# Experts' first and third matrices laid out by four consecutive rows to a partition, in a two-layer hybrid kernel with grouped experts

## The reference, cut to what matters

```python
def _moe(h, router_w, router_b, w1, w3, w2):
    ...
    for e in range(N_EXPERTS):
        hid = jax.nn.silu(t @ w1[e]) * (t @ w3[e])
        y = y + gates[:, e:e + 1] * (hid @ w2[e])
    ...
# before it, per layer:  h = _rmsnorm(x) * (1 + scale) + shift
# w1[e], w3[e]: 1024 x 256     w2[e]: 256 x 1024
```

## Time and profile before

| | us |
|---|---|
| median of three runs | 1369.6 |
| profiled execution, its own time | 1365.57 |
| span of its profile | 1363.9 |
| PE busy in the span | 1225.5 (90%) |
| DVE / ACT / GpSimd busy | 841.9 / 477.0 / 322.9 |
| bytes moved by DMA | 234.77 MB in 125291 packets |
| of the packets, under 2 KB / under 8 KB | 77168 / 125200 |

### The profile page before, as it was taken

The page is one execution under the profiler, slowest core; times in us unless marked ns, Lnnn a source line. Parts: engine busy times, 40 slices in busy tenths (PEclk is TensorE's granted clock), DMA queues, the critical chain, the costliest instruction groups (busy, mean ns, idle before and its releaser), DMA issues.

```text
span 1363.9 us, 24844 instructions
## 1 busy us (share of the span) xinstructions
PE 1225.5 (90%) x9304; PEld 825.2 (61%) x9304; DVE 841.9 (62%) x1644; ACT 477.0 (35%) x974; POOL 322.9 (24%) x384
## 2 busy tenths in 40 slices
PE   2989999999799998699999699999999997899980
PEld 2478867847455453584854478888887555455540
DVE  5577575483566664869335677777774325576664
ACT  4000126203366551201038544444443102556541
POOL 1000009100233333100002433443443000333323
PEclk9899899899899999799999899999999998899995
DMA  9677666482999986311110000000001634599945
GB/s 365 217 247 284 213 233 219 134 304 101 319 378 324 378 287 203 125 62 62 62 62 0 31 3 3 21 3 2 3 2 64 233 106 154 200 383 378 380 132 206
DMA packets 125291, 234.77 MB, mean 172 GB/s; under 512 B 9376, under 2 KB 77168, under 8 KB 125200
## 3 DMA queue, kind: packets, MB, share of 16 engines
q1 hardware_dynamic: 114464, 200.42, 42.3%
q0 software_dynamic: 10560, 33.04, 6.8%
q10 hardware_dynamic: 176, 0.05, 0.0%
HBM read 210.42 MB, written 23.07 MB: 171 GB/s over the span
## 4 chain that ended last, share of the span: by engine, by line
PE 67%; DVE 13%; SPq 9%; DMA 5%; issue 4%; ACT 2%; POOL 1%; DVEq 0%; POOLq 0%; ACTq 0%
PE PS L2191 14%; PE PS L2157 8%; SPq L735 8%; PE PS L2336 7%; PE PS L2112 5%; PE PS L2354 3%; PE PS L2535 2%; PE PS L2085 2%; PE PS L2517 2%; PE PS L2423 2%; PE PS L2486 2%; DMA arena<-in_ada_w 2%; DVE arena L1390 2%; DVE arena L1762 2%; PE PS L2261 1%
## 5 line engine op out<-in xcount | busy, mean ns | idle before, releaser
L2336 PE MATMUL PS<-WR,arena 128*64 128x256 f32 x1536 | 180.0, 388 | 5.9 <-ACT arena L1188 4.5
L2336 PEld LDWEIGHTS PS<-WR,arena 128*64 128x64 f32 x1536 | 109.3, 139 | 61.2 <-ACT arena L1188 7.2
L2191 PE MATMUL PS<-WR,arena 128*128 128x256 f32 x480 | 111.4, 393 | 4.3 <-DVE arena L1837 4.2
L2157 PE MATMUL PS<-WR,arena 128*128 128x512 f32 x256 | 113.6, 600 | 0.0
L1390 DVE SCALAR_TENSOR_TENSOR arena<-arena,cact 128x1024 f32<-128x1024 f32 x77 | 99.4, 1291 | 12.1 <-DMA arena<-in_ada_w 6.0
L2191 PEld LDWEIGHTS PS<-WR,arena 128*128 128x128 f32 x480 | 94.0, 197 | 20.2 <-DVE arena L1837 3.4
L1640 DVE COPY WR<-arena 128x2560 f32 x48 | 71.9, 1498 | 38.5 <-issue 26.0
L2354 PE MATMUL PS<-W,arena 128*64 128x512 f32 x384 | 92.9, 604 | 0.9 <-DVE arena L1666 0.9
L923 POOL DMA_DIRECT2D expert_rows<-arena x92 | 49.7, 540 | 157.6 <-DVE arena L1674 150.8
L1172 ACT COPY WR<-arena 128x1536 f32 x48 | 71.0, 1480 | 44.8 <-issue 26.5
L2112 PE MATMUL PS<-arena,WR 128*128 128x512 f32 x192 | 85.5, 601 | 1.1 <-DVE arena L1477 1.1
(11 more groups left out here) (382 smaller groups left out, 2231.0 us busy)
## 6 DMA issues: line engine op xcount, KB each, us to landing
arena<-in_moe_w SPq DMA_DIRECT2D x96, 1024.0 KB, 13.1
arena<-in_ada_w SPq DMA_DIRECT2D x82, 512.0 KB, 4.7
WR<-in_rwkv_w_rkv SPq DMA_DIRECT2D x6, 2048.0 KB, 8.0
expert_rows<-arena POOLq DMA_DIRECT2D x92, 128.0 KB, 5.5
WR<-in_mix_w_in SPq DMA_DIRECT2D x5, 2048.0 KB, 10.5
WR<-in_mix_w_out SPq DMA_DIRECT2D x2, 2048.0 KB, 7.9
expert_rows<-arena SPq DMA_DIRECT2D x1, 4096.0 KB, 14.7
xn_rows<-WR SPq DMA_DIRECT2D x2, 2048.0 KB, 7.2
```

The costliest lines, as they stand in the source:

```text
L2157: last = mm(out, HT[:, c, b * P:(b + 1) * P], WR[:, (first_tile + half) % 2, c, :], start=(c == 0), stop=(c == KC - 1))
L2191: last = mm(out[:, n * 256:n * 256 + 256], left, right, start=(c == 0), stop=(c == 3))
L2336: last = mm(PS[rows2[h], 2 + n, 0:2 * P].rearrange("p (m f) -> p m f", m=2), XgT[:, n, c, :], w[:, :, c, cols(h)], start=(c == 0), stop=(c ...
```

## The change

The loads of w1 and w3 give a partition two runs of four consecutive rows (4 KB each), one run from each half of the 1024 features. Chunk number 4h + c then holds the features 512h + 4p + c in place of 512h + 128c + p. `turn` picks each fourth column of the gathered rows to match. Since scale and shift are now needed in the same order, SP rewrites sixteen columns of `MOD` for each layer (`reorder`): one transfer to DRAM, number by number, a wait for its landing, and one transfer back, into a part of `vecA`. ACT and DVE wait for that once in each layer. w2 and all else stay as they are.

```diff
+        mod_dram = nc.dram_tensor("mod_rows", (2 * D,), F32, kind="Internal").ap()
+        MODP = [vecA[:, 24 * (2 * layer + 1):24 * (2 * layer + 1) + 2 * KC] for layer in range(2)]
...
+            def reorder(layer):
+                sp.wait_ge(sem("mod_ready"), 2 * layer + 3)
+                sp.wait_ge(sem("sgu_in"), 32 + 32 * layer)
+                with nc.allow_non_contiguous_dma(reason="one number of each partition"):
+                    sp.dma_start(mod_dram.rearrange("(j p) -> p j", p=P), MOD[:, 2 * layer + 1, 0:2 * KC]
+                                 ).then_inc(sem("sgu_in"), 16)
+                sp.wait_ge(sem("sgu_in"), 48 + 32 * layer)
+                sp.dma_start(MODP[layer].rearrange("p (m h c) -> p m h c", m=2, h=2),
+                             mod_dram.rearrange("(m h p c) -> p m h c", m=2, h=2, c=4)).then_inc(sem("sgu_in"), 16)
...
             sp.wait_ge(*free("s4", 4))
+            reorder(0)
             sp.dma_start(y_dram[NEXP * ROWS:MAX_ITEMS * ROWS, :].rearrange("(k p) f -> p k f", p=P),
...
-                    for k, name in enumerate(("moe_w1", "moe_w3", "moe_w2")):
-                        sp.dma_start(slot[:, k * 2048:(k + 1) * 2048].rearrange("p (c f) -> p c f", c=2 if k == 2 else KC),
-                                     io[name][layer, e].rearrange("(c p) f -> p c f", p=P)
+                    for k, name in enumerate(("moe_w1", "moe_w3")):
+                        sp.dma_start(slot[:, k * 2048:(k + 1) * 2048].rearrange("p (h f) -> p h f", h=2),
+                                     io[name][layer, e].rearrange("(h p c) f -> p h (c f)", h=2, p=P)
                                      ).then_inc(sem(f"ring_in{e % SLOTS}"), 16)
+                    sp.dma_start(slot[:, UP:EXPW].rearrange("p (c f) -> p c f", c=2),
+                                 io["moe_w2"][layer, e].rearrange("(c p) f -> p c f", p=P)
+                                 ).then_inc(sem(f"ring_in{e % SLOTS}"), 16)
...
             moe(0)
+            reorder(1)
             sp.dma_start(W1L, io["rwkv_w1"][0].rearrange("(c p) f -> p c f", p=P)).then_inc(sem("lora_in"), 16)
...
+                act.wait_ge(sem("sgu_in"), 64 + 32 * layer)
                 act.wait_ge(sem("items"), layer + 1)
...
-                                                    bias=MOD[:, L, c:c + 1], scale=MOD[:, L, 8 + c:9 + c])
+                                                    bias=MODP[layer][:, c:c + 1], scale=MODP[layer][:, 8 + c:9 + c])
...
+                v.wait_ge(sem("sgu_in"), 64 + 32 * layer)
                 stage_up(0, expert(0))
...
-                        last = nc.tensor.transpose(PS[:, n + c // 2 * 4, cols(c % 2)], Xg[:, n, cols(c)], ident[:, :])
+                        last = nc.tensor.transpose(PS[:, n + c // 2 * 4, cols(c % 2)],
+                                                   Xg[:, n, :].rearrange("p (q c) -> p c q", c=4)[:, c, :], ident[:, :])
```

More of the change, by code:

```diff
@@ L1653, in turned @@
                         at = (c % 4 - 2) * P + c // 4 * ROWS
-                        last = ts(XgT[:, n, c, :], PS[:, 4 + n, at:at + ROWS], MOD[:, L, 8 + c:9 + c],
-                                  MOD[:, L, c:c + 1], ALU.mult, ALU.add)
+                        last = ts(XgT[:, n, c, :], PS[:, 4 + n, at:at + ROWS], MODP[layer][:, 8 + c:9 + c],
+                                  MODP[layer][:, c:c + 1], ALU.mult, ALU.add)
                     last.then_inc(M("xgv_hid"), 1)
```

## The result

The changed kernel takes 1374.44 us (median of 6 runs, 1370.65 to 1375.51), the kernel before 1368.74 beside it (6 runs, 1367.0 to 1371.43). The ratio is 1.0042, with a 95% interval of 1.0029 to 1.0055: longer by 0.42%, 5.7 us, where I had forecast 5.9 us less. The time lies inside the range (1359.5 to 1378.0), but on the side that I gave 0.18.

What follows compares the result with a forecast made beforehand. PE and DMA were both near their limit in the expert stages, with 6.7 us due to late weights. Terms -6.4 + 0 + 0.5 = -5.9 us took 1369.6 to 1363.7 us (-0.43%), range 1359.5 to 1378.

Steps and rivals of the forecast that it cites:

- The loads, -6.4 us: Expert stages: longer runs for w1 and w3 land weights sooner; -3.0 - 1.7 - 1.7 = -6.4 us.
- Both waits: PE waits for late weights, 3.30 us in layer 0 and 1.72 in layer 1; booked as -3.0 and -1.7 us.
- the slower item: Layer 0 item behind the late expert, 1.69 us over the pace at a lower PE clock; booked as gone.
- Rival B: Expert loops: slower item stays or experts behind the late one come late; 1366.4 us, within 0.3%; chance 0.20.
- "Cost 0" for the second `reorder`: Behind layer 0's experts: SP waits for the landing but reaches `tile(7)` in time; 0 us.
- "+0.5" for its small pieces: Gathers after layer 0: small pieces take up to 4 us, later small matrices return 1.4; +0.5 us booked.
- Rival C: Second `reorder`: 4-byte pieces take 20 us to land and delay gathers; +4 us, 1367.2 us, within 0.3%; chance 0.07.
- The return of 1.4 us: Gathers after layer 0: small matrices now come later, which can give back 1.4 us.
- "I take 0" for the turns: PE's transposes: stepped weight loads hide behind the 110 ns spacing; 0 us, upper bound +19.6 us.
- Rival A: PE's turns: stepped load is slow, transposes over 110 ns apart; 1383.3 us at 212 ns; chance 0.18.
- Rival D: Expert loops: longer runs delay an item's gathers past 10.2 us; 1381.7 us at 11 us; chance 0.05.
- The first `reorder`, 0: Ahead of the store at 223.32 us: 3 to 15 us of SP delay, some 20 us of cover; 0 us.

Runs made afterwards that it cites:

- the fourth kernel: The changed kernel with the second `reorder` moved some 250 us later, behind the loads at about 772 us: 1365.96 us, ratio 0.9986 to the kernel before.

## Why the prediction was wrong

**The loads, -6.4 us: right.** Both waits went, the slower item with them, and alone the loads gave 5.9 us. The waits themselves aren't fixed numbers: in the profiles of four kernels with the old loads (both `reorder`s alone, small reads, spread writes, small matrices moved) the late expert of layer 0 is 3.8 to 4.3 us late and none is late in layer 1, so 5.4 to 5.9 us with the slower item would be the term there in place of 6.7. Rival B (less is returned) isn't borne out by the changed kernel or by the loads alone; a trace of it shows in three later kernels, where one `up` of layer 0 waits 0.2 to 0.95 us for weights. The rule that I quoted from the Trainium skill, "DMA: Bandwidth & Descriptors", section "Why small descriptors are slow" (7% between the two lengths of run in place of 14%) would have made the sum 1.5 us smaller; the measurement of the loads alone lies between the two sums, 6.4 and 4.9 us, and its interval (3.8 to 7.9 us) excludes neither.

**"Cost 0" for the second `reorder`, and "+0.5" for its small pieces: the step that failed most.** The landing time lay within its bounds of 3 to 15 us (10.4; measured 13.7), and the way of the damage was named, small pieces beside the gathers. Its size was not: bounds of -1.4 to +4 us against 7.3 measured alone and 9.3 in the profile. I priced pieces by number, from reads of 64 bytes, and capped the delay by how much longer they would be under way. But the row of the router matrix is a read from DRAM, and this is a write to it. 2048 reads of 4 bytes held up no gather, and 128 writes of 64 bytes had landed before the gather that counts; 2048 writes of 4 bytes side by side took every gather beside them to 16.5 to 18.0 us, from 5.1 to 8.2. The gathers landed 6 to 7 us after these writes did, as if they had waited for them, and not later by the difference of two landings. Rival C had this mechanism, with its sign "a last lower gather over 9 us" (17.3), but priced it at 4 us, and so stood on the wrong side of zero. The return of 1.4 us for small matrices that come later is real, as the kernel with these alone moved shows (2.2 us off the gather), but what holds the gathers up is stronger.

**"I take 0" for the turns: the second step that failed.** The row that I leaned on, matmuls 106 ns apart behind plain weight loads of 192 ns, was taken to say that any load of about that length hides behind a spacing of 106 to 110. I had also called the contiguous load twice as fast as the plain one, while the row reads 142 against 192 ns, a third apart. The stepped load measured 209 ns, and the turn grew by 0.09 us. Four loads grew by 4 x 67 = 268 ns, and a third of that, 0.09 us, came through to PE; how the rest is hidden no row shows. The bounds (0 to 0.102 us a transpose) held the truth, 0.023 us a transpose, near their lower end. This is Rival A, with its sign (a turn over 0.6 us), at a fifth of the price that I gave it. The slowing is less than a factor of two, as that rival's "against" had it; that it would then hide was the error. The sentence from the Trainium skill, "Advanced Engine Details and Errata", section "SBUF Cachelines", which I quoted under Rival A, names a penalty for such a step, and the trace agrees, 209 ns against 142.

**Gathers in the loop (Rival D): refuted.** No item waits in either loop.

**The first `reorder`, 0: right,** by the cover of the modulation loads. The added waits of ACT and DVE show no cost: the fourth kernel has both in, and its -0.14% is what loads and turns leave.

So the two prices together, +11.6 us, exceed the 5.9 that the loads bring, while with the step alone 1.6 us of gain are left, and with the `reorder` alone the 7.3 us measured would have left 1.4 us of loss, less than can be told from no change.

## What to carry to other kernels

When a layout change saves on one side of a matmul, price the step where it lands: a load on the critical engine pays for it on each item, while a producer with slack pays once, off the path. Don't write to DRAM number by number beside transfers that someone waits for: write each partition's numbers as one run and let the reading side be the scattered one, or put the transfer where nobody waits for what runs beside it. And price a transfer by a row of the same direction: a read says nothing about a write.

## What the runs showed of the hardware

- In the expert loops a weight load of 128 columns in fp32 for a transpose takes 140 to 142 ns from contiguous columns, 207 with a step of two, 209 with a step of four; 0.09 us of each four is not hidden.
- 2048 writes of 4 bytes to neighbouring places in DRAM land after 12.2 to 13.7 us in the changed kernel and in the one with both `reorder`s alone, and after 14.1 us at 770 us, where no gathers run; spread 64 bytes apart over 128 KB, after 6.0 to 6.9; the same bytes in 128 runs of 64, after 1.9 to 3.2.
- The last lower gather beside such neighbouring writes takes 15.9 to 17.3 us, beside the spread ones 8.6, beside the small matrices 8.0, with nothing beside it 5.8. While the neighbouring writes were under way in the changed kernel, DMA moved 33 GB/s.
- 2048 reads of 4 bytes from DRAM land after 2.9 us at 227 us, where no gathers run, and after 14.1 beside the gathers, which take 6.6 us then.
- Three small matrices, issued at the moment of the gathers, lengthen the last lower one from 5.8 to 8.0 us; the kernel without them there is 3.0 us faster.
- ACT takes 2117 ns to read 1024 numbers of each partition with a step of four and write them contiguously, 2033 ns to read them contiguously and write them apart, 1132 ns without a step on either side.
